# Turning units' rows and inner values in 32x32 blocks on VectorE, in a two-layer mixture-of-experts backbone

## What is computed

```python
def grouped_moe(h, router_w, router_b, w_gate, w_up, w_down):
    aff = jax.nn.sigmoid((h @ router_w).astype(jnp.float32))
    ...                                   # one of 4 groups, then top 2 of its 4 experts; weights sum to 1
    y = jnp.zeros_like(h)
    for e in range(N_EXPERTS):
        he = jax.nn.silu(h @ w_gate[e]) * (h @ w_up[e])
        y = y + combine[..., e:e + 1] * (he @ w_down[e])
    return y
```

## Time and profile before

| | us |
|---|---|
| median of 3 runs (974.53, 974.70, 975.36) | 974.7 |
| the profiled execution | 974.29 |
| its span, first to last instruction | 972.4 |
| PE busy | 846.4 (87%) |
| PEld busy | 452.2 (47%) |
| DVE busy | 443.4 (46%) |
| ACT busy | 176.7 (18%) |
| mean granted TensorE clock | 0.927 of full speed |
| HBM read over the span | 291.39 MB |

### The profile page before, as it was taken

The page is one execution under the profiler, slowest core; times in us unless marked ns, Lnnn a source line. Parts: engine busy times, 40 slices in busy tenths (PEclk is TensorE's granted clock), DMA queues, the critical chain, the costliest instruction groups (busy, mean ns, idle before and its releaser), DMA issues.

```text
span 972.4 us, 19946 instructions
## 1 busy us (share of the span) xinstructions
PE 846.4 (87%) x7838; PEld 452.2 (47%) x7839; DVE 443.4 (46%) x1119; ACT 176.7 (18%) x383; POOL 32.8 (3%) x58
## 2 busy tenths in 40 slices
PE   8899989998979867998678996799878989799784
PEld 3544636444554434554234553374435545445342
DVE  3266879866889851222011332433542222223316
ACT  3221111225631201011001110240211110101001
POOL 0100000110001000000000001000000000000010
PEclk9699999997999898999779998799899999989988
DMA  9989976999005798449999799994559699999971
GB/s 340 362 302 331 336 284 250 331 331 347 0 1 219 289 380 355 193 177 418 418 418 416 301 377 413 392 416 183 213 217 390 253 412 417 420 417 419 416 294 44
DMA packets 89963, 303.64 MB, mean 312 GB/s; under 512 B 9072, under 2 KB 16288, under 8 KB 73456
## 3 DMA queue, kind: packets, MB, share of 16 engines
q1 hardware_dynamic: 75648, 282.49, 74.0%
q0 software_dynamic: 3552, 12.59, 3.4%
q10 hardware_dynamic: 10704, 7.75, 2.5%
HBM read 291.39 MB, written 14.68 MB: 315 GB/s over the span
## 4 chain that ended last, share of the span: by engine, by line
PE 61%; DVE 12%; DMA 12%; SPq 9%; issue 4%; ACT 2%; ACTq 0%; DVEq 0%
PE bank L1836 16%; DMA raw<-in_w_up 9%; PE bank L1849 8%; PE bank L1610 7%; SPq L484 7%; PE bank L1799 4%; PE bank L1600 3%; PE bank L1752 3%; PE bank L2017 3%; PE bank L1823 2%; PE bank L1614 2%; DMA consts_sb<-in_constants 2%; PE bank L1815 2%; PE bank L1619 1%; PE bank L1546 1%
## 5 line engine op out<-in xcount | busy, mean ns | idle before, releaser
L1836 PE MATMUL bank<-raw,arena 128*32 128x256 f32 x3392 | 227.3, 410 | 40.1 <-DMA raw<-in_w_up 28.3
L1836 PEld LDWEIGHTS bank<-raw,arena 128*32 128x32 f32 x3392 | 112.6, 116 | 133.6 <-DMA raw<-in_w_up 39.8
L1370 DVE TENSOR_TENSOR arena<-arena,bank 64x256 f32<-64x256 f32 x53 | 22.5, 425 | 246.8 <-ACT arena L805 246.8
L1849 PE MATMUL bank<-raw,arena 128*32 128x256 f32 x1696 | 109.4, 399 | 13.8 <-DVE arena L1358 11.4
L1849 PEld LDWEIGHTS bank<-raw,arena 128*32 128x32 f32 x1696 | 52.1, 113 | 53.5 <-issue 15.5
L805 ACT ACTIVATE arena<-bank 64x256 f32<-64x256 f32 x53 | 19.9, 376 | 275.2 <-PE bank L1836 275.2
L1610 PE MATMUL bank<-ring,arena 128*128 128x512 f32 x160 | 69.9, 594 | 0.0
L1799 PE MATMUL bank<-arena 128*32 128x256 f32 x912 | 60.7, 384 | 2.7 <-DVE arena L1281 2.7
L913 DVE SCALAR_TENSOR_TENSOR bias<-ring,small,bias 128x512 f32<-128x512 f32 x77 | 57.9, 752 | 2.7
L1823 PE MATMUL bank<-consts_sb,arena 64*128 64x64 f32 x212 | 35.6, 289 | 23.2 <-issue 21.9
L1823 PEld LDWEIGHTS bank<-consts_sb,arena 64*128 64x128 f32 x212 | 28.2, 191 | 47.2 <-issue 45.2
(11 more groups left out here) (275 smaller groups left out, 915.0 us busy)
## 6 DMA issues: line engine op xcount, KB each, us to landing
raw<-in_w_gate SPq DMA_DIRECT2D x64, 1024.0 KB, 18.6
raw<-in_w_up SPq DMA_DIRECT2D x64, 1024.0 KB, 19.3
raw<-in_w_down SPq DMA_DIRECT2D x64, 1024.0 KB, 20.5
ring<-in_ada_w SPq DMA_DIRECT2D x24, 2048.0 KB, 13.3
ring<-in_w_in SPq DMA_DIRECT2D x7, 2048.0 KB, 13.6
unit_results<-arena ACTq DMA_DIRECT2D x220, 32.0 KB, 5.4
ring<-in_w_out SPq DMA_DIRECT2D x2, 2048.0 KB, 21.9
ring<-in_w_fnet SPq DMA_DIRECT2D x2, 2048.0 KB, 16.2
```

What stands on the lines that cost most here:

```text
L1836: ins = mm(ps[4][o:o + S, 0:FW], xT[:, i, j * S:(j + 1) * S], w[:, k % 4, h * FW:(h + 1) * FW], start=(k == 0), stop=(k == KD - 1))
L1849: ins = mm(ps[5][j * S:(j + 1) * S, 0:XW], hT_e[:, k % QN, k // QN * S:(k // QN + 1) * S], w[:, k % 2, j * XW:(j + 1) * XW], start=(k == 0 ...
```

## The change

What it does, part by part:

- **Rows.** `turn_x` and ScalarE's copy to `xs` go. `turned` becomes one VectorE transpose, in blocks of 32x32, from the bank of the gather to `xT`: block s,k of the read is column 8s+k, so partition 32j+s of `xT` holds row 256j+8s+k of x for each k, which is row 8p+k of partition p.
- **Gate and up.** `gate_up` still makes 32 products of 256 columns, but each takes 128 columns of gate and 128 of up (one access with two pieces, from two buffers side by side, `pairs`), for four column groups of the array. Bank 4 then holds gate in columns 0 to 127 and up in 128 to 255, on all partitions. It waits for a gate half and an up half together. Silu and product work on 128x128.
- **Inner values.** `turn_he` and `turn_back` go; `turn_h` is one VectorE transpose of `he`, in blocks, from SBUF to SBUF, after the result of the unit before. Row 4p+k of the down matrix then has to be on partition p, so the down halves are loaded like the others, two neighbouring rows (8 KB) per partition and half.
- **Order.** VectorE: product(n), turned(n+1), result(n-1), turn_h(n), choose(n+3). TensorE: gate_up(n), down(n-1), gather(n+2), where the gather also waits for `xT_ready`, since `turned` now reads bank 6 itself.
- **Norm.** `by_k` goes: the normalised tokens are written in natural order, and the router's weights are loaded to match.

```diff
@@ -474,13 +470,9 @@
                 src = wt[l, e:e + 1, :, :]
-                if kind == "down":
-                    src = src.rearrange("e (k p) n -> p (e k) n", p=P)[:, hf * (KF // 2):(hf + 1) * (KF // 2), :]
-                    dst = halves[s][:].rearrange("p (k n) -> p k n", k=KF // 2)
-                else:
-                    src = src.rearrange("e (p k) n -> p (e k n)", k=KD)[:, hf * HW_:(hf + 1) * HW_]
-                    src = src.rearrange("p (a n) -> p a n", a=2)
-                    dst = halves[s][:].rearrange("p (a n) -> p a n", a=2)
+                src = src.rearrange("e (p k) n -> p (e k n)", p=P)[:, hf * HW_:(hf + 1) * HW_]
+                src = src.rearrange("p (a n) -> p a n", a=2)
+                dst = halves[s].rearrange("p (a n) -> p a n", a=2)
...
@@ -802,9 +794,7 @@
                     act.wait_ge(E["gate_up_done"], n + 1)
-                    nc.scalar.activation(sg[64:P, :], ps[4][0:64, 0:FW], ACT.Silu).then_inc(E["silu_done"], 1)
-                    act.wait_ge(E["x_in_psum"], n + 3)
-                    nc.scalar.copy(xs, ps[6][:, 0:XW]).then_inc(E["x_ready"], 1)
+                    nc.scalar.activation(sg, ps[4][:, 0:FW], ACT.Silu).then_inc(E["silu_done"], 1)
...
@@ -1178,15 +1166,11 @@
                 link(nc.vector.reciprocal(rstd[:, 4 + t:5 + t], rstd[:, t:t + 1]))
-                even = squares[:, t, :] if by_k else f_[:, t, :]
+                even = f_[:, t, :]
...
                     link(ins)
-                    if by_k:
-                        ins = nc.vector.tensor_tensor(f_kd[t], even.rearrange("p (m k) -> p m k", k=KD),
-                                                      shift.rearrange("p (m k) -> p m k", k=KD), ALU.add)
-                    else:
-                        ins = nc.vector.tensor_tensor(even, even, shift, ALU.add)
+                    ins = nc.vector.tensor_tensor(even, even, shift, ALU.add)
...
@@ -1332,11 +1316,11 @@
-                def turned(n):
-                    dve.wait_ge(E["xT_in_psum"], n + 1)
-                    nc.vector.tensor_copy(xT.rearrange("p i n -> p (i n)"), ps[7][:, 0:XW]
-                                          ).then_inc(E["xT_ready"], 1)
+                def turned(n, bank=6):
+                    dve.wait_ge(E["x_in_psum"], n + 1)
+                    nc.vector.transpose(xT, ps[bank][:, 0:XW].rearrange("p (s k) -> p k s", k=KD)
+                                        ).then_inc(E["xT_ready"], 1)
...
@@ -1352,11 +1336,12 @@
-                def turn_back(n):
-                    dve.wait_ge(E["hT_in_psum"], n + 1)
-                    nc.vector.tensor_copy(hT_e, ps[7][:, XW:XW + QN * 64].rearrange(
-                        "p (q n) -> p q n", q=QN)).then_inc(E["hT_ready"], 1)
+                def turn_h(n, first=False):
+                    if not first:
+                        dve.wait_ge(E["y_in_psum"], n)
+                    dve.wait_ge(E["he_ready"], n + 1)
+                    nc.vector.transpose(hT_e, he.rearrange("p (s k) -> p k s", k=KF)).then_inc(E["hT_ready"], 1)
...
@@ -1367,7 +1352,7 @@
                     dve.wait_ge(E["silu_done"], n + 1)
-                    nc.vector.tensor_tensor(he[64:P, :], sg[64:P, :], ps[4][64:P, 0:FW], ALU.mult
+                    nc.vector.tensor_tensor(he, sg, ps[4][:, FW:2 * FW], ALU.mult
...
@@ -1377,10 +1362,10 @@
                     n = dve.snap(units, min_val=1, max_val=MAX_UNITS)
-                    turn_back(n - 1)
...
                     result(n - 1, place, stores)
+                    turn_h(n)
...
@@ -1394,18 +1379,14 @@
-                for n in range(2):
-                    dve.wait_ge(E["x_in_psum"], n + 1)
-                    if n:
-                        dve.wait_ge(E["xT_in_psum"], n)
-                    nc.vector.tensor_copy(xs, ps[n][:, 0:XW]).then_inc(E["x_ready"], 1)
-                turned(0)
+                turned(0, 0)
...
                 product(0)
-                turned(1)
+                turned(1, 1)
+                turn_h(0, True)
...
@@ -1806,37 +1786,20 @@
                     pe.wait_ge(E["chosen_ready"], n - 1)
+                    pe.wait_ge(E["xT_ready"], n)
...
-                def turn_x(n):
-                    pe.wait_ge(E["x_ready"], n + 1)
-                    for i in range(XI):
-                        ins = nc.tensor.transpose(ps[7][:, i * P:(i + 1) * P], xs[:, i * P:(i + 1) * P], ident)
-                    ins.then_inc(E["xT_in_psum"], 1)
-                def turn_he(n):
-                    pe.wait_ge(E["he_ready"], n + 1)
-                    pe.wait_ge(E["xT_ready"], n + 2)
-                    for q in range(QN):
-                        ins = mm(ps[7][:, XW + q * 64:XW + (q + 1) * 64], he[64:P, q * P:(q + 1) * P], ident[64:P, 64:P],
-                                 start=True, stop=True)
-                    ins.then_inc(E["hT_in_psum"], 1)
...
                     for k in range(KD):
-                        i, j = k % XI, k // XI
-                        for m, kind in enumerate(("gate", "up")):
-                            w = half(kind, k // 4, k % 4 == 0).rearrange("p (k n) -> p k n", k=KD // 2)
-                            for h in range(HH):
-                                o = 64 * m + S * h
-                                ins = mm(ps[4][o:o + S, 0:FW], xT[:, i, j * S:(j + 1) * S],
-                                         w[:, k % 4, h * FW:(h + 1) * FW], start=(k == 0), stop=(k == KD - 1))
-                                if begins and (k, m, h) == (0, 0, 0):
-                                    ins.then_inc(E["expert_begun"], 1)
+                        w = half("gate", k // 4, k % 4 == 0).rearrange("p (m k n) -> p k m n", m=2, k=KD // 2)
+                        for j in range(JN):
+                            ins = mm(ps[4][j * S:(j + 1) * S, 0:2 * FW].rearrange("p (m n) -> p m n", m=2),
+                                     xT[:, k, :], w[:, k % 4, :, j * FW:(j + 1) * FW], start=(k == 0),
+                                     stop=(k == KD - 1))
+                            if begins and (k, j) == (0, 0):
+                                ins.then_inc(E["expert_begun"], 1)
...
@@ -1846,7 +1809,7 @@
                         for j in range(JN):
-                            ins = mm(ps[5][j * S:(j + 1) * S, 0:XW], hT_e[:, k % QN, k // QN * S:(k // QN + 1) * S],
+                            ins = mm(ps[5][j * S:(j + 1) * S, 0:XW], hT_e[:, k, :],
...
@@ -1854,9 +1817,14 @@
                         s = raw_slot(l, par, HALVES.index((kind, hf)))
+                        if kind == "gate":
+                            if due:
+                                pe.wait_ge(full[s], raw_fill(l, s, pr))
+                                pe.wait_ge(full[s + 1], raw_fill(l, s + 1, pr))
+                            return pairs[s // 2][:]
...
                             pe.wait_ge(full[s], raw_fill(l, s, pr))
-                        return halves[s][:]
+                        return halves[s]
...
@@ -1866,10 +1834,7 @@
                     n = pe.snap(units, min_val=1, max_val=MAX_UNITS)
-                    turn_he(n - 1)
                     gate_up(n, own, begins)
-                    pe.wait_ge(E["hT_ready"], n)
-                    turn_x(n + 1)
...
@@ -1937,29 +1899,23 @@
                     n = pe.snap(units, min_val=1, max_val=MAX_UNITS)
-                    turn_he(n - 1)
...
                     gate_up(n, own, True)
-                    turn_x(n + 1)
...
                             n = pe.snap(units, min_val=1, max_val=MAX_UNITS)
-                            turn_he(n - 1)
...
                             down(n - 1, own)
-                            turn_x(n + 1)
...
                 n = pe.snap(units, min_val=NE, max_val=MAX_UNITS)
-                turn_he(n - 1)
...
                 if l == 0:
-                    pe.wait_ge(E["x_ready"], n + 2)
...
```

44 lines of the change are left out of this document (17 added, 27 removed).

## The result

| | before | after |
|---|---|---|
| median, us | 975.0 (4 runs, 974.5 to 975.7) | 940.75 (4 runs, 938.1 to 945.0) |
| the profiled execution, us | 974.29 | 944.97 |
| its span, us | 972.4 | 943.2 |

The profiled execution after was the longest of the four, 4.2 us over their median; what follows compares it with the profiled one before, so of the 13.3 us between the forecast of 954 and the median the profile can explain 9.0.

The account below looks back on a forecast made before the run. TensorE and transfers were taken to bound the kernel in turn, as a relay, so saved TensorE time counts only where transfers stand still. Layer 0 -12.9 and layer 1 -7.3 total -20.2 from 974.29, forecast 954 us, range 943 to 964.

Parts of the forecast that it names:

- TensorE's turns, 0.96 per unit: Each unit on TensorE loses turn_x (0.37 us) and turn_he (0.59 us), 0.96 us together, and keeps 6.31.
- 18 counted steps: Unit steps where the saved TensorE time was taken to shorten the run: 13 in layer 0, 5 in layer 1.
- Down loads, 0: Two neighbouring rows per partition in packets of the same size: no change in load pace, bounds -1% and +1%.
- The end of layer 0: Layer 0's last experts: last up weights at 594.1 us, gate and up of expert 15 ending at 598.1, before 610.41.
- the collision: Layer 0's end: GpSimd's fetch of stored results runs beside expert 15's weights, which lose 28% over 8.9 us, 3.5 us.
- the gap of 5.83 us: TensorE's issue time ahead of layer 0's last down, taken as unchanged at 5.83 us.
- transfers bind less: Rival, chance 0.17: fetch disturbs nothing, half of the layer's branch gaps run beside the new waits; 947 us.
- Between the layers, -2.1: From layer 0's last down to layer 1's first gate product: norm 0.70 us and start of experts 1.36 us saved.
- Start of a layer, -1.36: Before a layer's first gate product: copy, turn, copy go, VectorE's turn runs beside the second gather; 1.36 us saved.
- the new wait there, 1.24: Layer 0, before expert 1: the second turned queues behind weigh, product and silu, so TensorE waits 1.24 us.
- the turn's cover: Down before the gather, 1.75 us, hides the chain to the gather; VectorE's turn may take 0.94 us before TensorE waits.
- Layer 1, -5.2 from its first gate product: Layer 1's experts: five unit starts at 0.96 us and 2.23 at the end saved, fetch 1.4 and eight rounds 0.4 lost.

## Why the prediction was wrong, point by point

- **TensorE's turns, 0.96 per unit.** The step that failed first. I read each step from its start to the next one's and took the other steps as unchanged; they were longer because of the turns. Measured 1.23. Over the 18 counted steps that is 4.9 us: 0.27 x 13 = 3.5 in layer 0, where load 13 came 3.4 early beyond the sum, and 1.4 in layer 1. That 3.5 and 3.4 agree is in part luck: the down loads gave 0.7 up to there as well, and at load 5 only 1.2 of 1.9 had arrived.
- **Down loads, 0.** "In packets of the same size" was wrong: two distant rows are two packets of 4 KB. The bound of 1% was the truth (15.23 for 15.38 us per expert), about 1.8 us in layer 0.
- **The end of layer 0.** The last up half came 48.3 us after load 13, forecast 48.7; the collision cost 3.1, forecast 3.5. The step held, its price partly by luck: the fetch was issued at 576.66, not at the estimated 581.7, and lay beside the weights for 10.4 us of their undisturbed time, not 8.9, which by the same 28% would have made 4.0. But I kept the gap of 5.83 us ahead of the last down, and it was 1.66, and from none to 1.66 in eight profiles with this TensorE list; 4.66 with the turns put back. That is 4.2 us that I could not price, and the rival "transfers bind less" had given too little for it. Together with load 13's 3.4 and gate and up at a higher clock (3.37 for 4.0) it makes 8.2 of the 9.3; the other 1.1 I did not price. This is the second step that failed, an idle time carried over unchanged; what sets its length stays open.
- **Between the layers, -2.1.** Measured -4.2: the norm's 1.75 instead of 0.70, the start's 1.46 for 1.36, and the modulation sums behind the last down, 3.85 for 4.88 us at a higher clock. In layer 0's profile the norm's gain was lost to the clock (25.6 us for 24.6 up to the first gather).
- **Start of a layer, -1.36; the new wait there, 1.24; the turn's cover.** Right: the first gate product came 1.76 us after the gather for 3.22 before, the wait was 1.24 us, and the turn may take 0.88 for 0.94. The turn at 0.44 (taken: 0.45) hides. The Trainium skill's rule on PSUM reads (Advanced Engine Details and Errata, Memory Cachelines) would have had this read, a stride of eight floats, pay: the trace does not agree, 0.443 us against 0.42 for the plain copy of that size; no run here reads the bank in order by a transpose. `turn_h` took 0.40 us, above its bound of 0.37, and nobody waited for it.
- **Layer 1, -5.2 from its first gate product.** Measured -2.8. The saved turns arrived (7.27 to 6.04 per unit), but the gap in front of expert 2's products was 5.18 us instead of 2.67 and 1.55, and expert 1 began later behind the new wait, part of it at half clock (5.10 us for gate and up instead of about 3.8). At load 5, 1.9 of the 2.4 are missing. From load 5 to the last up weights it took 172.4 us, 0.7 less than forecast, and from there to the end 38.1 (38.7 before, forecast 36.9), 1.2 more, with the gather and the gate and up behind the wait partly at half clock (1.93 and 4.93 us).
- **Gate and up in two pieces, 0.** Right: 3.46 us, less than the 3.59 of before by the seam alone. The late gap of 4.32 us went, as forecast, and a wait for weights took its place.

The direction and the relay of TensorE and transfers were right. Of the 9.0 us in the profile, 9.3 came up to the last down of layer 0 and 2.1 between the layers, against 2.4 lost in layer 1. The turns (4.9) and the down loads (1.8) were mis-sized terms whose sizes only a run shows; they overlap with the losses above and don't simply add to the 9.0. The branch gap (4.2) and what the clock gave back (0.6, and 1.0 at the modulation sums) no row of before could have given. The other 4.2 us up to the median are the distance of the profiled execution from it.

## What to carry to other kernels

A step's price on a pipelined engine is the change of the period when it goes, not the time between its start and the next: what its neighbours lose at its borders comes on top (here 0.14 us, where the weight loader stood 0.41), and only a run with the step alone put back or taken out gives its size. Where a kernel passes the limit back and forth between engine and transfers, follow the points at which the limit changes hands; then each term can be checked by itself, as here, even when the total is off. And idle time removed from TensorE can be worth more than its length (1.75 us for 0.65 in layer 1), or nothing (layer 0), by the clock behind it.

## What was not expected of the hardware

- Between products of 32 columns on TensorE, two 128x128 transposes or two 64x64 products cost 0.14 and 0.13 us beyond the time from their start to their successor's (0.51 for 0.37, 0.72 for 0.59).
- A 32x32-block transpose of 128x256 floats by VectorE takes 0.443 us from PSUM, with a step of 0.33 to 0.37 when they follow one another; one of 128x128 within SBUF takes 0.40, nearly the same for half the size.
- The unexplained gap of TensorE in front of expert 1 of layer 0 was 5.24 us with the transfers silent and 5.27 with the list shifted by 64 instructions, for 5.21 and 6.54 in the two profiles without either: neither of the two moved it beyond what it varies by itself.
- Packets of 8 KB instead of 4 for a third of the weights: 422 instead of 418 GB/s where the transfers set the pace.
